# Two norms finished piece by piece, and eleven merge tiles in three split passes

## What is computed

```python
ada = einsum('bd,de->be', c, w_ada) + b_ada              # 2048 x 12288
sh1, sc1, gt1, sh2, sc2, gt2 = split(ada, 6)
h = rmsnorm(x, norm1_w) * (1.0 + sc1) + sh1
proj = einsum('btd,de->bte', h, w_in)                    # q, kv, gates, dn_qkv, a, b, z, merge
...
g_nsa, g_dn = split(sigmoid(merge), 2)
mixed = g_nsa * (o_nsa @ w_br_a) + g_dn * (o_dn @ w_br_b)
x = x + gt1 * (mixed @ w_out)
h2 = rmsnorm(x, norm2_w) * (1.0 + sc2) + sh2
x = x + gt2 * peer(h2)                                   # 16384 experts, 16 of them for each of 8 heads
```

## Time and profile before

| | |
|---|---|
| median of the runs | 3137.82 us |
| the profiled execution's own time | 3127.99 us |
| its span, first to last instruction | 3125.1 us |
| mean granted clock of TensorE | 0.956 of full |
| busy: TensorE, VectorE, ScalarE | 2895.7, 1675.5, 954.3 us |
| moved | 707.21 MB, mean 226 GB/s |

### The profile page before, as it was taken

The page is one execution under the profiler, slowest core; times in us unless marked ns, Lnnn a source line. Parts: engine busy times, 40 slices in busy tenths (PEclk is TensorE's granted clock), DMA queues, the critical chain, the costliest instruction groups (busy, mean ns, idle before and its releaser), DMA issues.

```text
span 3125.1 us, 42601 instructions
## 1 busy us (share of the span) xinstructions
PE 2895.7 (93%) x16484; PEld 2440.7 (78%) x16484; DVE 1675.5 (54%) x2748; ACT 954.3 (31%) x1257; POOL 18.6 (1%) x21
## 2 busy tenths in 40 slices
PE   4799998887688899997999999999999999999999
PEld 2587786666586686997988888888888888888887
DVE  0345564415423200655359877777655666666665
ACT  1001012312120210333311355555433444444443
POOL 0000000000000000000000000000000000000000
PEclk8899998998796899998999999999999999999999
DMA  9677655464110667553434565656986888878884
GB/s 397 254 260 248 235 230 193 158 201 174 61 55 34 257 253 304 208 190 135 162 140 172 181 227 216 228 216 229 370 330 248 295 290 288 285 282 290 293 292 171
DMA packets 192810, 707.21 MB, mean 226 GB/s; under 512 B 21942, under 2 KB 137270, under 8 KB 156086
## 3 DMA queue, kind: packets, MB, share of 16 engines
q1 hardware_dynamic: 181030, 671.96, 58.6%
q0 software_dynamic: 2304, 16.78, 1.4%
q10 hardware_dynamic: 9360, 16.85, 1.4%
HBM read 662.82 MB, written 51.09 MB: 228 GB/s over the span
## 4 chain that ended last, share of the span: by engine, by line
PE 87%; DVE 5%; DMA 4%; SPq 2%; ACT 1%; issue 1%; DVEq 0%; ACTq 0%
PE psum L572 16%; PE psum L1098 12%; PE psum L1148 7%; PE psum L1147 7%; PE psum L1149 7%; PE psum L1099 6%; PE psum L1057 5%; PE psum L973 3%; PE psum L974 3%; PE psum L975 3%; DMA ring<-in_w_ada 3%; PE psum L551 2%; PE psum L1078 2%; PE psum L738 1%; PE psum L790 1%
## 5 line engine op out<-in xcount | busy, mean ns | idle before, releaser
L2113 DVE TENSOR_TENSOR w_lo<-ring,w_hi 128x1024 fp32r<-128x1024 f32 x464 | 545.3, 1220 | 196.7 <-ACT w_hi L1519 196.4
L1098 PE MATMUL psum<-h_both,w_hi 128*128 128x512 f32 x1664 | 593.1, 399 | 1.2 <-DVE h_both L2129 1.2
L572 PE MATMUL psum<-hT,ring 128*128 128x264 f32 x2304 | 535.9, 394 | 10.7 <-DVE xT L1907 5.5
L572 PEld LDWEIGHTS psum<-hT,ring 128*128 128x128 f32 x2304 | 443.7, 194 | 98.5 <-issue 16.2
L1099 PE MATMUL psum<-h_both,w_lo 128*128 128x256 f32 x1664 | 466.0, 280 | 0.0
L1519 ACT ACTIVATE w_hi<-ring 128x1024 fp32r<-128x1024 f32 x464 | 451.9, 1045 | 32.8 <-ACT CK L1506 25.6
L1147 PE MATMUL psum<-w_hi,acts 128*128 128x512 f32 x1024 | 398.5, 389 | 0.0
L1149 PE MATMUL psum<-w_hi,acts 128*128 128x512 f32 x1024 | 398.4, 389 | 0.0
L1148 PE MATMUL psum<-w_lo,acts 128*128 128x512 f32 x1024 | 398.3, 389 | 0.0
L1098 PEld LDWEIGHTS psum<-h_both,w_hi 128*128 128x128 f32 x1664 | 312.7, 188 | 79.4 <-issue 7.9
L1099 PEld LDWEIGHTS psum<-h_both,w_lo 128*128 128x128 f32 x1664 | 313.1, 188 | 0.0
(11 more groups left out here) (424 smaller groups left out, 3632.5 us busy)
## 6 DMA issues: line engine op xcount, KB each, us to landing
ring<-in_w_peer_u SPq DMA_DIRECT2D x64, 2048.0 KB, 8.2
ring<-in_w_peer_v SPq DMA_DIRECT2D x64, 2048.0 KB, 7.8
ring<-in_w_ada SPq DMA_DIRECT2D x48, 2048.0 KB, 11.5
ring<-in_w_in SPq DMA_DIRECT2D x42, 2048.0 KB, 7.8
arena<-gelu_scratch SPq DMA_DIRECT2D x64, 512.0 KB, 8.5
arena<-route_w SPq DMA_DIRECT2D x64, 512.0 KB, 9.4
ring<-in_cache_cmp SPq DMA_DIRECT2D x64, 256.0 KB, 4.1
ring<-in_cache_slc SPq DMA_DIRECT2D x128, 128.0 KB, 2.2
```

The costliest lines, as they stand in the source:

```text
L572: mm = pe.matmul(bank[b + j][:, 0:NT], w[:, k, j * P:(j + 1) * P], hT[:, k, :], start=(k == 0), stop=(k == KT - 1))
L1098: pe.matmul(out, top[:, k, c], h2_both[:, :, k, 0:SEQ], start=k == 0, stop=False)
L2113: dve.tensor_tensor(w_lo[:, s, cols], ring[:, s, cols], w_hi[:, s % 2, cols], ALU.subtract).then_inc(S["expert_lo"], 1)
```

## The change

**First norm.** The loads of the condition tiles no longer wait for the constants, and come alternately from the shift and the gain half. The sum of squares, the root, the reciprocal and one multiply over all groups go ahead of the condition tiles. After every second tile VectorE makes the gain of two groups and shifts them; TensorE multiplies the small projection pair by pair behind the next tiles. **Merge.** After dn_out ScalarE copies hT, rounded, into merge_hi (the memory of o_hi), VectorE leaves the rest in place of hT, and the eleven tiles run as three passes; the tops and rests of a tile's weights are made two tiles ahead. The copies into o_hi move behind the eleventh tile. **Second norm.** `modulate` runs in four groups of four; the tops, rests and the first w_peer_q tile wait group by group; the gain is made ahead of the root.

```diff
+N_MERGE_LATE = N_MERGE // 2 - N_MERGE_EARLY - 1
...
+        merge_hi = o_hi
...
-            sp.wait_ge(S["consts_in"], 16 * 6)
-
             with sp.Fori(0, N_ADA0 // 4) as i:
                 for s in range(4):
-                    load(s, i, tile_of("w_ada", 4 * i + s))
+                    load(s, i, tile_of("w_ada", 2 * i + s // 2 + 8 * (s % 2)))
+            sp.wait_ge(S["consts_in"], 16 * 6)
...
-            with pe.Fori(0, N_ADA0 // 4) as i:
-                for s in range(4):
-                    ada_main(s, i)
-                    ada_reduce(s, 4 * i + s)
-
             for k in range(KT):
                 pe.wait_ge(S["x_squared"], k // 4 + 1)
                 mm = pe.matmul(bank[7][:, 0:NT], ones[:], hT[:, k, :], start=(k == 0), stop=(k == KT - 1))
             mm.then_inc(S["x_summed"], 1)
-            pe.wait_ge(S["h_ready"], 1)
+
+            def small_pair(p):
+
+                pe.wait_ge(S["h_ready"], p + 1)
+                for k in (2 * p, 2 * p + 1):
+                    mm = pe.matmul(bank[7][0:SM, 0:NT], wsmall[:, k, :], hT[:, k, :], start=(k == 0), stop=(k == KT - 1))
+                if p == KT // 2 - 1:
+                    mm.then_inc(S["small_mm"], 1)
+
             pe.wait_ge(S["wsmall_in"], 16)
-            for k in range(KT):
-                mm = pe.matmul(bank[7][0:SM, 0:NT], wsmall[:, k, :], hT[:, k, :], start=(k == 0), stop=(k == KT - 1))
-            mm.then_inc(S["small_mm"], 1)
+            for m in range(N_ADA0):
+                ada_main(m % 4, m // 4)
+                ada_reduce(m % 4, m)
+                if m % 2 and m >= 3:
+                    small_pair((m - 3) // 2)
+            small_pair(KT // 2 - 1)
...
+            def late_merge(m):
+
+                s, b = m % 2 * 2, m % 2 * 2
+                for j in range(2):
+                    pe.wait_ge(S["proj_evac"], T_END + 2 * (m + N_MERGE_EARLY + 1) + j + 1)
+                    for k in range(KT):
+                        if j == 0 and k % 4 == 0:
+                            pe.wait_ge(S["merge_lo"], 4 * m + k // 4 + 1)
+                        c = slice(k % 4 * 256 + j * P, k % 4 * 256 + (j + 1) * P)
+                        mm = three_pass(bank[b + j][:, 0:NT], w_lo[:, s, k * 256 + j * P:k * 256 + (j + 1) * P], dense_hi(m % 2, k // 4)[:, c],
+                                        h2_lo[:, k, :], merge_hi[:, k, :], k == 0, k == KT - 1)
+                    mm.then_inc(slot_used[s] if j else S["proj_mm"], 1)
+
+            for m in range(N_MERGE_LATE):
+                s = 1 if m % 2 else 3
+                if m % 2 == 0:
+                    ada_main(3, 20 + m // 2, PAGED[3])
+                late_merge(m)
+                ada_reduce(s, N_ADA1 + m)
+                if m % 2 == 0:
+                    ada_main(1, 21 + m // 2, PAGED[1])
+            ada_reduce(1, N_ADA1 + N_MERGE_LATE)
...
-            pe.wait_ge(S["o_split"], 8)
             for n in range(8):
-                dense(16 + n, "pq_evac", hq_lo, hq_hi)
+                dense(16 + n, "pq_evac", hq_lo, hq_hi, 4 if n == 0 else 0)
...
+            act.wait_ge(S["x_summed"], 1)
+            act.wait_ge(S["consts_set"], 3)
+            act.activation(rstd[:], bank[7][:, 0:NT], ACT.Sqrt, bias=epst[:], scale=1.0 / D).then_inc(S["x_std"], 1)
             with act.Fori(0, N_ADA0 // 4) as i:
                 for s in range(4):
                     ada_copy(s, i)
...
             act.wait_ge(S["dn_out"], 1)
+            act.wait_ge(slot_used[2], 22)
+            for k in range(0, KT, 4):
+                act.activation(merge_hi[:, k:k + 4, :], hT[:, k:k + 4, :], ACT.Copy).then_inc(S["merge_hi"], 1)
+
+            def merge_top(m):
+
+                s, use = m % 2 * 2, 21 + m // 2
+                act.wait_ge(slot_full[s], 16 * (use + 1 - PAGED[s]))
+                for c in range(4):
+                    act.activation(dense_hi(m % 2, c), ring[:, s, c * SLOT // 4:(c + 1) * SLOT // 4], ACT.Copy).then_inc(S["merge_hi"], 1)
+
+            merge_top(0)
+            merge_top(1)
+            for m in range(N_MERGE_LATE):
+                s, use = m % 2 * 2, 21 + m // 2
+                ada_copy(1 if m % 2 else 3, 20 + (m + 1) // 2)
+                evacuate(s, use, H + 10 + 2 * m if m < 9 else T_Z + 2 * (m - 9), T_END // 2 + N_MERGE_EARLY + 1 + m, s, ACT.Sigmoid)
+                if m + 2 < N_MERGE_LATE:
+                    merge_top(m + 2)
+            ada_copy(1, 26)
             for k in range(0, 2 * H, 4):
                 t = k if k < H else T_DNV + k - H
                 act.activation(o_hi[:, k:k + 4, :], PR[:, t:t + 4, :], ACT.Copy).then_inc(S["o_top"], 1)
...
-            act.wait_ge(S["h_ready"], 2)
             for k in range(0, KT, 4):
+                act.wait_ge(S["h_ready"], 9 + k // 4)
                 act.activation(hq_hi[:, k:k + 4, :], hT[:, k:k + 4, :], ACT.Copy).then_inc(S["o_top"], 1)
...
             dve.wait_ge(S["x_std"], 1)
-            dve.wait_ge(S["ada_done"], N_ADA0 + 1)
             step(dve.reciprocal(rstd[:], rstd[:]))
-            modulate(0, xT[:], hT[:], S["h_ready"])
+            step(dve.tensor_tensor(hT[:], xT[:], rstd[:].unsqueeze(1).broadcast_to((P, KT, NT)), ALU.mult))
+            for m in range(N_ADA0):
+                ada_bias(m, 2 * (m // 2) + 2 * (N_ADA0 // 2) * (m % 2))
+                if m % 2:
+                    dve.wait_ge(S["ada_done"], m + 2)
+                    gain(0, m - 1, 2)
+                    shift(0, m - 1, 2, hT)
...
+            for k in range(0, KT, 4):
+                dve.wait_ge(S["merge_hi"], k // 4 + 1)
+                dve.tensor_tensor(h2_lo[:, k:k + 4, :], hT[:, k:k + 4, :], merge_hi[:, k:k + 4, :], ALU.subtract)
+
+            def merge_rest(m):
...
+                    dve.wait_ge(S["merge_hi"], 4 * m + c + 5)
+                    dve.tensor_tensor(w_lo[:, s, cols], ring[:, s, cols], dense_hi(m % 2, c), ALU.subtract).then_inc(S["merge_lo"], 1)
+
+            merge_rest(0)
+            merge_rest(1)
+            for m in range(N_MERGE_LATE):
+                ada_bias(m + N_ADA1, 2 * (m + N_ADA1))
+                if m + 2 < N_MERGE_LATE:
+                    merge_rest(m + 2)
...
+            gain(1, 0, KT)
             dve.wait_ge(S["x_std"], 2)
             step(dve.reciprocal(rstd[:], rstd[:]))
             dve.wait_ge(S["x1_done"], 8)
-            modulate(1, xT[:], hT[:], S["h_ready"])
...
+            for k in range(0, KT, 4):
+                modulate(1, k, 4, xT, hT)
+                if k:
+                    h_low(k - 4)
+            h_low(KT - 4)
```

More of the change, by code:

```diff
@@ L952, in _, with three_pass @@
             pe.wait_ge(S["hn_std"], 6)
[L953 to L964, removed]
+            def three_pass(out, w, w_top, x, x_top, start, stop):
+                pe.matmul(out, w_top, x_top, start=start, stop=False)
+                pe.matmul(out, w, x_top, start=False, stop=False)
+                return pe.matmul(out, w_top, x, start=False, stop=stop)
+            def late_merge(m):
[18 more added lines that the diff above has]
+            ada_reduce(1, N_ADA1 + N_MERGE_LATE)
             for n, (s, use) in enumerate(LAST_ADA):
@@ L970, in _ @@
             pe.wait_ge(S["dn_out"], 1)
[L971 to L975, removed]
             def dense_tile(q, k, j):
@@ L1207, in _ @@
                     ada_copy(s, i)
-            act.wait_ge(S["x_summed"], 1)
-            act.wait_ge(S["consts_set"], 3)
-            act.activation(rstd[:], bank[7][:, 0:NT], ACT.Sqrt, bias=epst[:], scale=1.0 / D).then_inc(S["x_std"], 1)
             act.wait_ge(S["small_mm"], 1)
@@ L1612, in ada_bias, with modulate @@
                                   ALU.add).then_inc(S["ada_done"], 1)
-            with dve.Fori(0, N_ADA0) as m:
-                ada_bias(m, 2 * m)
-            def modulate(which, src, dst, ready):
-                sh, sc = 3 * KT * which, 3 * KT * which + KT
-                w = par("nw")[:, KT * which:KT * which + KT].unsqueeze(2).broadcast_to((P, KT, NR))
-                step(dve.scalar_tensor_tensor(A1[:], adaT[:, sc:sc + KT, :], 1.0, w, ALU.add, ALU.mult))
-                step(dve.tensor_tensor(dst, src, rstd[:].unsqueeze(1).broadcast_to((P, KT, NT)), ALU.mult))
-                step(dve.tensor_tensor(dst[:, :, SEQ:NT], dst[:, :, SEQ:NT], A1[:, :, 1:NR], ALU.mult))
-                dve.tensor_tensor(dst[:, :, SEQ:NT], dst[:, :, SEQ:NT], adaT[:, sh:sh + KT, 1:NR], ALU.add)
-                for k in range(KT):
-                    ins = dve.tensor_scalar(dst[:, k, 0:SEQ], dst[:, k, 0:SEQ], A1[:, k, 0:1], adaT[:, sh + k, 0:1],
+            def modulate(which, k, count, src, dst):
+                sh, ks = 3 * KT * which, slice(k, k + count)
+                step(dve.tensor_tensor(dst[:, ks, :], src[:, ks, :], rstd[:].unsqueeze(1).broadcast_to((P, count, NT)), ALU.mult))
+                shift(which, k, count, dst)
@@ new lines, in gain, with shift @@
+            def gain(which, k, count):
+                sc, ks = 3 * KT * which + KT, slice(k, k + count)
```

(9 more changed lines are left out.)

29 lines of the change are left out of this document (12 added, 17 removed).

## The result

The changed kernel took 3089.81 us (median of four runs, 3085.73 to 3096.21) beside 3137.72 us of the kernel before: a ratio of 0.9849, with 95% interval 0.983 to 0.9869, or 41 to 53 us. Forecast were 3095 us, between 3086 and 3110. A second comparison gave 3091.0 against 3138.37 us, 0.9849 again (0.9828 to 0.9871).

The account below looks back on a forecast made before the run. TensorE's own work, 87% of the span, was taken to bound the kernel. Gains of 24.8 + 13.7 + 4.4 = 42.9 us off 3137.82 gave 3095 us, range 3086 to 3110.

Parts of the forecast that it names:

- The forecast case: Whole kernel: all three parts gain as computed, 42.9 us together, giving 3095 us; chance 0.75.
- First norm, 24.8: Part one, first norm and page loop: second cache pages issued at 138.2 instead of 163.00, 24.8 us earlier.
- The choice between 24.8 and 27.0: Behind the first norm: 24.8 us if the cache pages bind, 27.0 if VectorE does not hold TensorE; 24.8 was taken.
- Late merge, 13.7: Part two, eleven merge tiles: first tile loses 13.4 us, ten others gain 27.1 at period 13.94, net 13.7 us.
- The slack of ScalarE's queue: Late merge: some 1.8 us left per tile; a weight load later than that costs its excess once a tile.
- Second norm, 4.4: Part three, second norm in four groups: TensorE's first w_peer_q tile starts earlier, in bursts; gain 4.4 us, between 2.8 and 5.9.
- the two clock cases: Second norm: third burst fast, gain 5.9 us; or every gap leaves the clock low, gain 2.8 us.
- the row of the load stretch: Profile row of the condition tile loads, bursts with waits at 0.78 of full clock; used to choose 4.4 us.
- The late merge did not give back: Rival: late merge gives back what it wins, break-even period 15.3 us; time 3108.6 us, chance 0.12.
- The page loop took nothing like half of part one: Rival: page loop, or TensorE falling behind the condition tiles, eats half the first norm's gain; 3107.4 us, chance 0.09.
- The split chain did not set the pace: Slower rival: load, split and tile stand one behind the other in the merge, 26.9 us a tile; 3225 us, chance 0.03.
- Everything behind is TensorE's, so the gains should last to the end: Stretches behind the changed parts: bound by TensorE's own work, so the summed 42.9 us should persist to the end.

Follow-up runs that it names:

- half the page work: Changed kernel, but VectorE multiplies only 8 of the 63 windows of each cache page set in the eight turns; 3082.22 us, ratio 0.9826.
- ten copies: Changed kernel, but ScalarE makes ten more copies of 128 columns ahead of each late merge tile's tops; late merge stage 411.2 us, mean period 15.98 us.
- the run with 3.67 us: Changed kernel, but VectorE makes two more reductions ahead of each of the second norm's first three subtractions; first w_peer_q copy 44.03 us after the sum's start.
- one fp32 tile: Changed kernel, but the first of eleven late merge tiles stays in fp32, the rest of hT made behind it; 3079.33 us, then 3080.16.
- the six reductions: Changed kernel, but VectorE makes six more reductions ahead of each of the second norm's first three subtractions; first w_peer_q copy 60.18 us after the sum's start.
- two and ten more copies: Changed kernel with two or ten more ScalarE copies of 128 columns ahead of each late merge tile's tops; that stage took 390.4 and 411.2 us.

## Why the prediction was right, and where its terms were off

The forecast case came true, 5 us lower than its figure: 47.4 to 47.9 us in the medians for 42.9 in the sum. By term:

**First norm, 24.8.** The steps hold to the tenth where they say when things happen: second pages at 138.2 (138.17), the first projection at 103.9 (102.50; 102.49 to 105.91 in other executions), no delay of the condition tiles. The choice between 24.8 and 27.0 rested on "a later part of the loop needs both engines", and that is what the traces show. TensorE was 28.4 us ahead (102.50 for 130.92) and kept that for six turns; the sets of pages were 24.8 to 25.3 us ahead; and at the head steps TensorE waited for VectorE, so that the end of the loop gained 25.3 us in this pair. Such waits were there before too (2.06 and 1.44 us at L605); with half the page work there is none. Among the nine traces with the new first norm and full pages the first of these waits lasts 1.5 to 5.3 us: 4.3 to 5.3 where the first projection starts at 102.50 to 103.06, 1.5 to 3.5 where it starts at 103.8 or later, while the head step itself starts at 316.7 to 319.3 in all. So most of TensorE's lead beyond the pages' is given back there. What was off is the size on the mean, 28.8. It was worked out against one trace: the three traces with the old norm issue the second set at 163.00, 164.52 and 166.41, the nine with the new one at 138.2 on the mean, 26.4 us earlier; what makes up the other 2.4 was not traced. The row sum and the multiply cost nothing, as assumed.

**Late merge, 13.7.** The first split tile started 1043.52 - 1035.07 = 8.45 us after the last DeltaNet product starts; the steps gave 1055.1 - 1046.75 = 8.35. The period was 14.03 for 13.94, which over ten tiles takes 0.9 us. Stage: -12.7 against two kernels with fp32 tiles, -13.8 with the trace of before included. The slack of ScalarE's queue, put at 1.8 us, measured 1.5 with ten copies; the wait left at L1222 is 0.6 to 1.3. The o_hi copies moved behind the eleventh tile stayed hidden: the branch products start 1231.33 - 1197.38 = 33.95 us behind that tile, 34.87 before.

**Second norm, 4.4.** This was mis-sized: -6.3, a little past the upper end of 5.9. Two things were off. VectorE's group took 2.92 us, not 3.2, so the last quarter was ready 18.3 us after the reciprocal began (at 1434.00) instead of 19.4. And between the two clock cases the middle was taken by the row of the load stretch; what came is the better one, with the third burst at full clock. There were two gaps where three were forecast: the last quarter was ready at 1449.82 + 2.49 = 1452.31, before the third burst was through. The rule of the Trainium skill (TensorE: Matmul & The Clock Gate, HAM oscillation), read in the prediction as a cost of every gap, speaks of bursts between waits of several us. This kernel's gaps of 1.10 us lie outside it, and the run with 3.67 us shows what it describes.

**The rivals.** The late merge did not give back; the ten-copies run shows how near it was. The page loop took nothing like half of part one. The split chain did not set the pace, since two slots and two buffers let ScalarE wait 8 us a tile for weights.

**What moved the sum.** On the means of the stages part one came out 4 us larger, part two between 1 smaller and even, part three 2 larger: 48.9 together, 6 more than forecast. That the medians came within 5 us of the forecast is therefore no proof of each term. "Everything behind is TensorE's, so the gains should last to the end" fell short by little: the two stages without changed code came out 2.1 and 2.4 us longer on the means, the first of them well within its spread from trace to trace; whether the second is the change's doing is not shown. All five stages come to 44.4, the medians to 47.4 and 47.9; a difference of 3 us is less than the second stage's spread. In the first pair 3.4 us were lost in the key products, at a lower clock. A kernel's own executions agree in that (the changed kernel's two have both groups long, the two with one fp32 tile the first only); but it comes with the merge alone and with the second norm alone, and not with the six reductions, so it hangs on no part of the change by itself. What decides it stays open.

## What to carry to other kernels

When work is split into pieces so that it starts earlier, ask what each engine can do in the wait that opens: here one tile left in the slower format filled 13 us that the faster one had to wait for its inputs. A stage that TensorE fills turn after turn can still be bound at its end, by a short instruction that stands behind a slow one in VectorE's queue; look for the first wait behind the full turns, not for idle time in them. And lay two executions of the same kernel beside each other before a stage that nobody changed is charged to a change.

## What the runs showed of the hardware that was not expected

- Execution to execution, one kernel's time moves with the mean granted clock: of 23 runs of the kernel before, the fastest took 3121.73 us at 0.958, the slowest 3146.72 at 0.950. The attention stretch, where TensorE waits often, has much of it: of the 11.1 us between the spans of the changed kernel's two traces (3094.4 and 3083.3) 8.6 arise there. Over all traces its 1844 matmuls, the same in every kernel, took 316.0 to 328.4 us.
- Short gaps do not keep the clock down. In three of the eight traces with gaps of 1.10 us it rose some 7 us behind the start of the first burst. In the other five (half the pages, two and ten more copies, both with an fp32 tile) it rose some 3 us behind it, so that the second burst ran at full clock, and it stayed at 1.00 over the gap of 2.4 us that followed, as here in the first with an fp32 tile. With gaps of 3.67 us it stayed at 0.50 into the third burst, in one execution.

```profile
1413.34 0.56 PE L963 MATMUL psum<-hq_hi,wd_hi 128*128 128x264 f32 x1 [9.68 <-DVE hq_lo L2109]
...
1417.42 0.36 PE L963 MATMUL psum<-hq_hi,wd_hi 128*128 128x264 f32 x1 [1.10 <-DVE hq_lo L2109]
...
1421.50 0.36 PE L963 MATMUL psum<-hq_hi,wd_hi 128*128 128x264 f32 x1 [2.38 <-DVE hq_lo L2109]
```

- The end of the second norm did not move with the clock's rise: 34.20 to 34.22 us in eight executions, whichever burst the rise fell into, since in all of them the third burst waits for its quarter from VectorE and runs at full clock.
